# Eight gate loads of the second block: from plain float32 products to three products of halves

## The reference

```python
h = rmsnorm(x, pre_norm_mix)
g_a, g_b, qa, ka, va, cq, ckv, kr = split(h @ w_in)      # g_a, g_b: 256 x 1024 each
out_a = sliding_window_attention(qa, ka, va)             # 8 heads
out_b = latent_attention(cq, ckv, kr)                    # 8 heads
merged = sigmoid(g_a) * (out_a @ w_o_a) + sigmoid(g_b) * (out_b @ w_o_b)
x = x + rmsnorm(merged @ w_out)
x = x + rmsnorm(relu(h2 @ w_up)**2 @ w_down)             # h2 = rmsnorm(x)
```

## Time and profile before

| | us |
|---|---|
| median of 3 runs (1543.12 to 1548.83) | 1548.81 |
| the profiled execution, its own time | 1548.97 |
| its span, first to last instruction | 1547.1 |
| second block's front, plain projections ahead of the loop | 1107.6 to 1137.1 |
| attention loop, turns 0 to 18 | 1137.1 to 1254.7 |
| oa and ob tiles | 1254.7 to 1284.8 |

### The profile page before, as it was taken

One profiled execution on the slowest core, in us unless ns is written; L12 is line 12 of the kernel. 1 busy time (PEld: TensorE's weight loads), 2 busy tenths in 40 slices (PEclk: granted clock), 3 DMA queues, 4 the chain that ended last, 5 costly groups with the idle time before them and its releaser, 6 DMA issues.

```text
span 1547.1 us, 26121 instructions
## 1 busy us (share of the span) xinstructions
PE 1354.9 (88%) x10156; PEld 1291.4 (83%) x10156; DVE 962.3 (62%) x2039; ACT 523.5 (34%) x990; POOL 580.8 (38%) x352
## 2 busy tenths in 40 slices
PE   7999999899898968696978886888899988799996
PEld 6989999898897868696978876878777878689996
DVE  4688955755378585858585758655236435584563
ACT  6444444444443121121202221211245544344341
POOL 1377842221365545354535353544011012122220
PEclk9999999899999989898989898999999999899998
DMA  7445553442359999999999999999611333145450
GB/s 277 158 158 173 187 191 110 163 159 87 127 212 420 422 420 422 422 422 422 422 421 420 420 421 421 422 421 422 275 55 43 122 109 136 55 158 197 164 191 28
DMA packets 58071, 397.40 MB, mean 257 GB/s; under 512 B 6272, under 2 KB 9856, under 8 KB 10368
## 3 DMA queue, kind: packets, MB, share of 16 engines
q0 software_dynamic: 36864, 268.45, 41.8%
q1 hardware_dynamic: 21120, 127.76, 23.4%
HBM read 395.14 MB, written 1.05 MB: 256 GB/s over the span
## 4 chain that ended last, share of the span: by engine, by line
PE 50%; DMA 21%; DVE 13%; issue 9%; ACT 4%; POOL 3%; DVEq 0%; POOLq 0%; ACTq 0%
DMA rows_late<-peer_uv_dram,stage 21%; PE bank L675 11%; PE bank L676 11%; PE bank L677 11%; PE bank L662 6%; PE bank L863 5%; DVE rows_late L1788 3%; PE bank L706 2%; ACT w_hi L1055 2%; POOL w_lo L507 1%; POOL rows_late L605 1%; DVE hid L1970 1%; PE bank L767 1%; DVE w_lo L507 1%; DVE rstd L1380 1%
## 5 line engine op out<-in xcount | busy, mean ns | idle before, releaser
L507 POOL TENSOR_TENSOR w_lo<-raw,w_hi 128x2048 fp32r<-128x2048 f32 x53 | 246.1, 4645 | 526.7 <-ACT w_hi L1055 526.7
L863 PE MATMUL bank<-h_norm,rows_late 128*128 128x128 f32 x2816 | 330.6, 280 | 22.7 <-ACT h_norm L1221 22.7
L863 PEld LDWEIGHTS bank<-h_norm,rows_late 128*128 128x128 f32 x2816 | 327.2, 197 | 25.8 <-ACT h_norm L1221 25.8
L1788 DVE SCALAR_TENSOR_TENSOR rows_late<-rows_late,squares 128x1024 f32<-128x1024 f32 x176 | 213.8, 1229 | 134.7 <-DMA rows_late<-peer_uv_dram,stage 121.8
L863 PE MATMUL bank<-h_norm,rows_early 128*128 128x128 f32 x1280 | 180.6, 310 | 95.9 <-ACT h_norm L1221 94.6
L863 PEld LDWEIGHTS bank<-h_norm,rows_early 128*128 128x128 f32 x1280 | 173.9, 223 | 102.7 <-ACT h_norm L1221 100.6
L605 POOL DMA_INDIRECT rows_late<-peer_uv_dram,stage x165 | 197.6, 1198 | 125.1 <-PE bank L863 72.9
L675 PE MATMUL bank<-x_hi_a,w_hi 128*128 128x256 f32 x704 | 208.4, 296 | 16.8 <-DVE x_lo_a L1399 9.9
L675 PE MATMUL bank<-x_hi_b,w_hi 128*128 128x256 f32 x640 | 190.0, 297 | 29.2 <-POOL w_lo L507 10.4
L507 DVE TENSOR_TENSOR w_lo<-raw,w_hi 128x2048 fp32r<-128x2048 f32 x51 | 127.2, 2495 | 141.7 <-ACT w_hi L1055 139.1
L1055 ACT ACTIVATE w_hi<-raw 128x2048 fp32r<-128x2048 f32 x104 | 197.6, 1904 | 50.7 <-PE bank L677 50.2
(11 more groups left out here) (289 smaller groups left out, 2018.4 us busy)
## 6 DMA issues: line engine op xcount, KB each, us to landing
raw<-w_in_dram SPq DMA_DIRECT2D x28, 1024.0 KB, 4.9
raw<-w_up_dram SPq DMA_DIRECT2D x16, 1024.0 KB, 4.8
raw<-w_down_dram SPq DMA_DIRECT2D x16, 1024.0 KB, 4.8
rows_late<-w_in_dram SPq DMA_DIRECT2D x12, 1024.0 KB, 9.7
raw<-w_kv_dram SPq DMA_DIRECT2D x8, 1024.0 KB, 4.8
raw<-w_peer_q_dram SPq DMA_DIRECT2D x8, 1024.0 KB, 5.0
raw<-sc_w_out_dram SPq DMA_DIRECT2D x4, 1024.0 KB, 4.8
raw<-cf_w_pw_dram SPq DMA_DIRECT2D x4, 1024.0 KB, 4.7
```

What stands on the lines that cost most here:

```text
L507: api.tensor_tensor(ring(w_lo, i), ring(raw, i), ring(w_hi, i).bitcast(F32), ALU.subtract).then_inc(w_lo_ready[LO_BY[i][0]], 1)
L863: mm = nc.tensor.matmul(ct(Y_ACC[c][t // 4], t % 4, P), expert_rows(k)[:, D + t * P:D + (t + 1) * P], ct(diag, k % DIAGS, P), start=False, ...
L1788: w_.scalar_tensor_tensor(out=row, in0=row, scalar=1.0, in1=h_tok[:, c * D:(c + 1) * D], op0=ALU.mult, op1=ALU.mult, accum_out=pre[:, side ...
```

## The change

The seven other loads of the front stay plain. The eight gate loads go back to the ring: SP loads them into `raw`, ACT and DVE make their halves, and PE makes each gate tile from three products. The normalised activations h (eight tiles) are therefore split too, as "h2", two tiles in each of turns 1 to 4. ACT makes the high half of the first gate load in turn 3, DVE its low half in turn 4; those of the others are made by `ahead`, before the drain of a gate tile on ACT and at the end of the turn on DVE. By the same rule the halves behind the loop move: the first oa load's high half comes in turn 16 instead of 15 (its low half stays in DVE's turn 16), the second's high half in turn 17 instead of 18; its low half is POOL's in both kernels.

```diff
-WHOLE = range(BEFORE_GATHERS + 1, LOAD_OF["gb", 7] + 1)
+WHOLE = range(BEFORE_GATHERS + 1, LOAD_OF["ga", 0])
-WHOLE_SLOT = dict(zip(WHOLE, [*range(SLOTS), 0, 1, 2, 7, 8, 6]))
+WHOLE_SLOT = dict(zip(WHOLE, (0, 1, 2, 3, 4, 7, 8)))
...
+          "peer": ..., "h2": (8, 0, 0, ("xo", 7)), "oa": ...
...
@@ PE, beside_attention @@
                 for t in GATE_TILES.get(i, ()):
                     name, n = gate_tile(t)
-                    linear_whole(name, [n], "w_in_2", t // 2, 256, lo=(t % 2) * P)
+                    linear(name, [n], "w_in_2", t // 2, "h2", DT, 256, lo=(t % 2) * P)
@@ ACT, beside_attention @@
-                if i == 15:
-                    round_to(LOAD_OF["oa", 0])
+                if 1 <= i <= 4:
+                    for k in (2 * i - 2, 2 * i - 1):
+                        split_hi("h2", k, lambda k: act.wait_ge(h_ready, DT + k + 1), h_tile(k), by_chunk)
+                if i == 3:
+                    round_to(LOAD_OF["ga", 0])
                 elif i == 18:
                     ahead("oa", 0)
@@ DVE, beside_attention @@
+                if 1 <= i <= 4:
+                    for k in (2 * i - 2, 2 * i - 1):
+                        dve.wait_ge(x_hi_ready, split_count("h2", k))
+                        w_.tensor_tensor(by_chunk(ct(x_lo[0], k)), h_tile(k), by_chunk(ct(x_hi[0], k).bitcast(F32)),
+                                         ALU.subtract).then_inc(x_lo_ready, 1)
+                if i == 4:
+                    subtract_to(LOAD_OF["ga", 0])
+                for t in GATE_TILES.get(i, ()):
+                    if t % 2 == 0 and t < 14:
+                        ahead(*gate_tile(t))
...
-                elif i == 16:
-                    subtract_to(LOAD_OF["oa", 0])
```

More of the change, by code:

```diff
@@ L221 @@
           "merge": (8, 0, 0, ("sc", 7)), "xa": (8, 1, 0, ("pw", 7)), "o": (8, 0, 0, ("mix", 7)),
-          "peer": (8, 1, 0, ("q", 7)), "oa": (4, 1, 0, ("qb", 7)), "ob": (4, 1, 4, ("qb", 7)),
+          "peer": (8, 1, 0, ("q", 7)), "h2": (8, 0, 0, ("xo", 7)), "oa": (4, 1, 0, ("qb", 7)), "ob": (4, 1, 4, ("qb", 7)),
           "wo": (8, 0, 0, ("gb", 7)), "mlp": (8, 1, 0, ("ob", 7)), "hid0": (FH, 2, 0, None),
@@ L500, in wait_halves_free @@
             elif i - RING in WHOLE:
-                eng.wait_ge(acc_ready, max(LAST_TILE[OCCUPANT[at]] for at in slots_of(i)[1:]) + 1)
+                eng.wait_ge(acc_ready, max([LAST_TILE[OCCUPANT[at]] for at in slots_of(i)[1:] if at in OCCUPANT], default=0) + 1)
         def w_lo_split(eng, api, i):
@@ L535, in load_whole @@
                 n, at = i - WHOLE[0], WHOLE_SLOT[i]
[L536 to L539, removed]
+                sp.wait_ge(rows_free, NC * PH * TOPK - TOPK + DIAGS + ROWS_EARLY + max(at + 1, RING))
                 sp.dma_start(whole(i), T[name][b]).then_inc(whole_landed[at], 16)
@@ L1024, in square_tile, with split_hi @@
                 s.activation(ct(squares, k), ct(src, k), ACT.Square).then_inc(squared, 1)
-            def split_hi(x, k, ready, src, **scale):
+            def split_hi(x, k, ready, src, view=lambda tile: tile, **scale):
                 _, pair, first, reader = SPLITS[x]
@@ L1031, in split_hi @@
                 ready(k)
-                s.activation(ct(x_hi[pair], first + k), src, ACT.Copy, **scale).then_inc(x_hi_ready, 1)
+                s.activation(view(ct(x_hi[pair], first + k)), src, ACT.Copy, **scale).then_inc(x_hi_ready, 1)
             def split_all(x, ready, src, at=0):
```

## The result

| | before | after |
|---|---|---|
| median, us (lowest to highest, 20 runs each) | 1548.12 (1543.12 to 1553.96) | 1553.94 (1546.58 to 1558.36) |
| ratio to before, 95% interval | | 1.0036 (1.0025 to 1.0046) |
| profiled execution, its own time / span | 1548.97 / 1547.1 | 1556.08 / 1554.3 |
| scores of turn 0 start | 1137.14 | 1137.68 |
| loop: from there to the first oa tile | 117.5 | 130.1 |

The change costs 5.6 us (0.36% of 1548.1), within the half per cent and inside the range. The profiled execution stands 2.1 above the median. Between the two traces the loop is 12.6 longer, the stretch behind it 4.7 and the next 1.3 shorter, and turn 0 starts 0.5 later: 7.1, the difference of the two times.

A forecast was written before the change was run, and what follows sets the result against it. PE bounds the attention loop, with program order on ACT and DVE making it wait. 1548.97 + 9.5 (20.2 lost, 10.7 gained) - 4.4 - 1.5 = 1552.6, plus 0.6 for the clock: 1553.2 us, range 1545.5 to 1560.

The forecast's parts named there:

- shorter way into the next scores: Scores behind a gate tile: 0.11 us less paid 14 times, a gain between 0 and 1.6, taken whole.
- turn 3: PE waits 2.3 us because halves of h on ACT and DVE delay the front and the rotation of k.
- gate 0: First gate tile, turn 5: PE waits 3.8 us for the first gate load's low half on DVE.
- turns 6, 7: PE waits 1.75 and 2.2 us: gate 0 drained late by ACT, front of turn 6 late on DVE.
- turns 9, 11, 13, 15, 17: PE waits 1.1, 2.8, 1.8, 3.2 and 1.3 us, one load in two turns holding up the next front.
- half clock in the loop: A fall of PE's clock after the longest of the new waits, priced at 0.6 us.
- wait at the fifth oa tile: Behind the loop: PE's 5.21 us wait shrinks to 0.8 as POOL finishes before DVE begins, a gain of 4.4.
- order theory: In the loop, instructions cost by where they stand in each engine's program, delaying the next front, not by total load.
- the recurrence: Turn-by-turn count of the loop, each instruction starting when engine and waits allow; it gave 20.2 us of new PE waits.
- The clock rival: At least two of the four longest loop waits are followed by clock 0.50, costing 6 to 12 us: 1561; chance 0.22.
- The halves did not hide: Denies the rival that the halves hide in the loop's free DVE and ACT time: 1543 or 1538; chance 0.12.
- lock-out: Rival for the loop: DVE locked out, its low halves taking 4.99 us each, 1574; chance 0.03.

The follow-up runs named there:

- filler, 128 rows: Changed kernel plus 10.8 us of idle PE work in its waits, as products over all 128 rows: 1551.02 us, ratio 1.0017.
- filler, 32 rows: Changed kernel plus 7.1 us of idle PE work: repeated rotary products in turns 5 and 6 and one gate tile made twice: 1552.33 us, ratio 1.0028.
- late high half: Changed kernel with ACT making the second oa load's high half in turn 18 again, as before the change: 1558.91 us, ratio 1.0067.
- h split ahead: Changed kernel with the sixteen halves of h made right after h, ahead of the plain projections: 1547.46 us, ratio 0.9990.
- low halves later: Changed kernel with DVE's low halves of the loads moved a turn or more behind ACT's high halves: 1542.61 us, ratio 0.9963.
- both: Changed kernel with the halves of h made ahead of the projections and DVE's low halves of the loads in later turns: 1534.78 us, ratio 0.9907.
- both, three low halves moved: Kernel with both moves, its low halves of loads 1, 2 and 6 in turns 5, 7 and 15 instead of 6, 8 and 14: 1533.98 us, ratio 0.9906.

## Why the prediction was right

The forecast was 1553.2, the median is 1553.94. Its own steps against the traces:

| step | forecast | after |
|---|---|---|
| sixteen gate tiles | -9.1 | 2.88 a tile, as forecast |
| shorter way into the next scores | -1.6 | not there |
| turn 3 | +2.3 | +2.1 (scores of turn 4 from 1163.40 to 1166.04, less 0.54 at the start) |
| gate 0 | +3.8 | 3.76 |
| turns 6, 7 | +1.75, +2.2 | 0, 1.44 |
| turns 9, 11, 13, 15, 17 | +1.1, 2.8, 1.8, 3.2, 1.3 | 0, 1.46, 1.45, 2.79, 0 |
| half clock in the loop | +0.6 | 9.0 |
| loop in all | +10.1 | +12.6 |
| wait at the fifth oa tile, first to fifth oa tile | 0.8, -4.4 | 0.69, -4.7 |
| clock behind the loop | -1.5 | -1.3 |

**The start.** Turn 3 and gate 0 came within 0.2. Moving the split of h away removed both, as the order theory says.

**The later waits and the clock** are one item. The waits measure 13.0 us (12.75 more than before), where the recurrence had 20.2; the half clock takes 0.49 of 18.5 us, 9.0. When PE runs at half speed, the chain of front, exponents and normalisation catches up, and the wait due next isn't there: the clock is at half in turn 5 and turn 6 has no wait, in turn 7 and turn 9 has none, in turn 15 and turn 17 has none. Where the clock had not fallen, these waits are there:

| turn | forecast | after | clock not fallen ahead of it | in which run |
|---|---|---|---|---|
| 6 | 1.75 | 0 | 1.7, covered by filler | filler, 128 rows |
| 7 | 2.2 | 1.44 | 2.08 | filler, 128 rows |
| 9 | 1.1 | 0 | 0.82 | filler, 32 rows |
| 11 | 2.8 | 1.46 | 2.46 | filler, 32 rows |
| 17 | 1.3 | 0 | 1.00 | late high half |

With these values in place the waits would be 18.1 us, 17.9 more than before. That is an estimate, since the rows are of kernels that differ a little from the change. By it the three falls gave back 5.1 of their 9.0 us and cost 3.9.

So the mechanism of the waits was right and two sizes were not. The 20.2 was 2.3 too high, most of it 0.3 to 0.4 us in each wait from turn 9 on; the term "for a fall of the clock ... I add 0.6" was 3.3 too low. That the two together (12.75 + 9.0 = 21.7, against 20.2 + 0.6) missed by only 0.9 is in part luck. A third mis-sized term is the "gain between 0 and 1.6", of which I took all: the next scores pay 0.09 behind an fp32r tile too (2.97 - 2.88), 0.11 behind a plain one, so the turn is 4.85 and not 4.75. The reason I gave, that the fp32r weight loads are the shorter ones, is not in the traces either: at the full clock a weight load lasts 0.19 us in both kernels. 0.9 and 1.6 are the 2.5 by which the loop missed. With 0.5 at the start and 0.1 more gained behind the loop they put this execution 2.9 over the forecast. The median is only 0.7 over it; the mean clock of the whole span was 0.941 in this execution and 0.9435 on average over the twenty.

**The clock rival** (1559 to 1565) had its condition met, two and more waits followed by 0.50, and even what I named as proof of an error: "PE's clock at 0.50 for more than 5 us inside the loop". By that test the prediction had the clock wrong. The rival's time didn't come, for the reason that was given against it, that slack swallows part. It had priced falls as if nothing were given back. The prediction also said that the trace of before shows nothing for waits of 2 to 4 us in the loop. It shows one: in turn 1 PE waits 2.10 us for ACT's `k_b`, until 1149.98, and the clock stays at 1.00. The other eight traces have the same wait and the same clock. The Trainium skill ("TensorE: Matmul & The Clock Gate", the section on why this matters for your kernels) says that idle gaps between bursts of matmuls, when they are long enough, send the clock back to half. The trace agrees behind 3.76. Behind 2.79 the clock fell in one execution and held in the other, and it fell behind 1.44 and not behind 1.46 and 1.45.

**The other rivals.** The halves did not hide, although DVE was busy only 55% of the loop. No low half on DVE took over 2.30 (nine of them, median 2.29), POOL's was done at 1268.1 and DVE's next began at 1270.16: no lock-out. That the 4.99 of before is a collision was argued from one row; it is now shown by bringing it back, for 5.0 us. The Trainium skill ("SBUF — State Buffer", the section on who interferes with whom) says that a VectorE instruction with two SBUF inputs and a GpSimd instruction that reads SBUF take turns at a shared port, the later one waiting until the first is done. The run with the late high half agrees: 4.992 us beside POOL, of which 2.8 were until POOL's end, and 2.28 to 2.29 alone.

**The sum over all kernels.** Loop = 117.5 - 9.1 + PE's waits beyond the 2.3 of before (2.10 in turn 1, 0.21 in turn 3) + what the clock was below 1.00 (in stretches of 4 us) + the work added:

| | waits | clock | work | sum | loop measured | ratio |
|---|---|---|---|---|---|---|
| change | 12.8 | 10.2 | | 131.4 | 130.1 | 1.0036 |
| h split ahead | 7.4 | 5.1 | | 120.9 | 121.0 | 0.9990 |
| low halves later | 8.0 | 3.4 | | 119.8 | 119.7 | 0.9963 |
| both | 2.5 | 0 | | 110.9 | 111.4 | 0.9907 |
| both, three low halves moved | 1.6 | 0 | | 110.0 | 110.5 | 0.9906 |
| filler, 32 rows | 7.7 | 5.1 | 7.1 | 128.3 | 128.0 | 1.0028 |
| filler, 128 rows | 5.3 | 3.4 | 10.8 | 127.9 | 129.1 | 1.0017 |
| late high half (after the loop) | 14.0 | 6.8 | | 129.2 | 128.7 | 1.0067 |

(A low clock costs nothing while PE waits: in the first row 9.0 of the 10.2 lie in the three busy stretches.) The sum holds within 1.3 us everywhere, so nothing large is missing. With both edits the change is worth what it was made of: 1534.8 against 1548.1, of which the trace shows 6.1 in the loop, 4.7 and some 1.3 behind it.

**Open.** Which waits make the clock fall. Their length alone does not tell: the same 2.79 in turn 15 was followed by a fall in one execution of the change's loop and not in the other, and in turn 7 a wait of 1.44 was, where 1.46 and 1.45 in turns 11 and 13 were not. Turn 7 has rotary products of 32 rows behind its wait and the others have not, which fits the two fillers at gate 0, but no run isolates it, and the falls behind 2.14 and 2.46 in turn 11 have no such products near them. How many falls an execution gets may make part of the spread of the change (1546.6 to 1558.4, where the kernel with both edits has 1532.7 to 1536.3). Over its twenty executions the slower ones had the lower mean clock (0.949 in the fastest, 0.937 in the slowest, correlation -0.76). But the kernel before shows the same (-0.7 to -0.8 in two sets of runs), so the stages outside the loop have their part in it.

## What to carry to other kernels

On an engine that runs in program order, price an instruction by what stands behind it, not by its length or by the engine's free share: the halves of eight loads and of h cost some 22 us of waits and lost clock in one order and 2.5 in another, with DVE at most 63% busy in either loop. Where a producer and its consumer on another engine stand in the same turn, the second engine idles first and is late afterwards; a turn between them took that away here. And an instruction moved between engines' turns should be checked against the neighbour with which it shares time: here one high half a turn earlier was worth 5 us.

## What the hardware did that I had not expected

- The clock fell to 0.50 at 1177 while PE issued products of 32 rows by 96 columns without a gap (3.84 us from 1173.76), 0.4 us before the wait began, and stayed at 1.00 when products of 128 by 128 stood in the same place. It is one trace of each; in all four traces in which gate 0 waits without such products ahead of it the clock fell there.
- A good part of a fall came back as a wait less: of the 9.0 us of lost clock of three falls some 5 by the estimate above. Two executions of the same loop, with three falls and with two, differ by 1.4 us, where the third fall alone had PE at half speed for 6 us.
- The stage of gathers in front of this block ends up to 5.8 us apart from one execution to the next (turn 0 starts at 1131.9 to 1137.7, always 29.5 us behind the first plain projection), whatever follows it; differences of the whole time under that size need many runs or the length of the stage itself.
